# A three-part feed-forward kernel: gate weights loaded ahead of the down weights, up-weight sums moved beside the down product, three low parts moved from GpSimd to VectorE

## The reference, cut to what matters

```python
h = x + jnp.concatenate([pool_o, attn_o], axis=-1) @ w_out
hn = rms_norm(h, norm_ffn)
return h + (jax.nn.silu(hn @ w_gate) * (hn @ w_up)) @ w_down
```

## Time and profile before

| | |
|---|---|
| median of 3 runs | 2499.61 us (2497.76 to 2503.51) |
| profiled execution, its own time | 2495.08 us |
| span of its trace | 2493.3 us |
| busy share PE, DVE, ACT, POOL | 88%, 59%, 35%, 39% |
| mean granted TensorE clock | 0.947 |

### The profile page before, as it was taken

How to read it: one execution, slowest core, us unless ns; L and a number is a source line. 1 busy time by engine, 2 the same in 40 slices (tenths; PEclk the granted TensorE clock), 3 DMA queues, 4 the chain that set the end, 5 groups by cost and what they waited for, 6 DMA issues and landing times.

```text
span 2493.3 us, 33524 instructions
## 1 busy us (share of the span) xinstructions
PE 2186.0 (88%) x12454; PEld 1963.1 (79%) x12454; DVE 1477.0 (59%) x2118; ACT 884.4 (35%) x2149; POOL 974.1 (39%) x597
## 2 busy tenths in 40 slices
PE   7999999979999798888868888888886988889888
PEld 6888888758778787787767787787875878878877
DVE  5555665531235566666667666666667566656665
ACT  5666666422352223223223222223223332322221
POOL 1000000322254455445546444455545545544452
PEclk9999999989999899999989899999998999999999
DMA  5111110336552221122224212221113322112221
GB/s 162 35 37 37 44 38 22 102 110 197 191 181 79 85 68 51 51 76 68 60 74 144 74 51 62 75 68 51 51 60 118 112 63 68 52 51 62 74 68 64
DMA packets 236730, 195.59 MB, mean 78 GB/s; under 512 B 20749, under 2 KB 216122, under 8 KB 236570
## 3 DMA queue, kind: packets, MB, share of 16 engines
q1 hardware_dynamic: 236570, 193.46, 25.4%
HBM read 158.50 MB, written 35.03 MB: 78 GB/s over the span
## 4 chain that ended last, share of the span: by engine, by line
PE 57%; DMA 12%; DVE 11%; issue 11%; ACT 5%; SPq 2%; POOL 1%; ACTq 0%; DVEq 0%
PE ps L750 16%; PE ps L751 15%; PE ps L752 15%; DMA w_lo_raw<-in_w_gate 10%; DVE ws_lo_raw L1424 3%; PE ps L846 2%; DVE act_lo L1495 2%; SPq L438 2%; PE ps L820 1%; DVE aa L1485 1%; ACT w_hi L1167 1%; PE ps L941 1%; PE ps L832 1%; DVE act_hi L1493 1%; ACT act_hi L1202 1%
## 5 line engine op out<-in xcount | busy, mean ns | idle before, releaser
L750 PE MATMUL ps<-xs_hi,w_hi 128*128 128x352 f32 x1848 | 637.1, 345 | 228.9 <-DVE u L1459 115.0
L678 POOL TENSOR_TENSOR w_lo<-w_lo_raw,w_hi 128x512 fp32r<-128x512 f32 (+1 forms) x264 | 456.5, 1739 | 814.9 <-DVE ws_lo_raw L1424 733.5
L752 PE MATMUL ps<-xs_lo,w_hi 128*128 128x352 f32 x1848 | 624.6, 338 | 0.0
L750 PEld LDWEIGHTS ps<-xs_hi,w_hi 128*128 128x128 f32 x1848 | 373.6, 202 | 253.7 <-issue 151.0
L678 POOL TENSOR_TENSOR ws_lo<-ws_lo_raw,w_hi 128x512 fp32r<-128x512 f32 x264 | 392.0, 1495 | 63.9 <-DVE ws_lo_raw L1424 41.5
L1559 DVE TENSOR_TENSOR h<-ps,h 128x512 f32<-128x512 f32 (+1 forms) x396 | 272.4, 690 | 216.3 <-PE ps L752 213.9
L752 PEld LDWEIGHTS ps<-xs_lo,w_hi 128*128 128x128 f32 x1848 | 373.1, 202 | 0.0
L751 PE MATMUL ps<-xs_hi,ws_lo 128*128 128x352 f32 x1056 | 353.0, 334 | 0.0
L1424 DVE TENSOR_TENSOR ws_lo_raw<-w_lo_raw 128x512 f32<-128x512 f32 x132 | 201.6, 1527 | 178.7 <-DMA w_lo_raw<-in_w_gate 174.5
L750 PE MATMUL ps<-w_hi,act_hi 128*128 128x512 f32 x660 | 259.0, 392 | 25.9 <-issue 23.7
L751 PE MATMUL ps<-xs_hi,w_lo 128*128 128x352 f32 x792 | 271.2, 342 | 0.0
(11 more groups left out here) (125 smaller groups left out, 3376.0 us busy)
## 6 DMA issues: line engine op xcount, KB each, us to landing
w_lo_raw<-in_w_gate SPq DMA_DIRECT2D x66, 512.0 KB, 7.0
w_lo_raw<-in_w_up SPq DMA_DIRECT2D x66, 512.0 KB, 5.1
w_lo_raw<-in_w_down SPq DMA_DIRECT2D x66, 512.0 KB, 4.2
xload<-in_x_prompt SPq DMA_DIRECT2D x16, 512.0 KB, 4.2
mix_d<-o_st SPq DMA_DIRECT2D x64, 128.0 KB, 1.8
xt_lo_raw<-mix_d SPq DMA_DIRECT2D x16, 512.0 KB, 6.3
wg_hi_raw<-in_x_prompt SPq DMA_DIRECT2D x16, 512.0 KB, 6.8
h_d<-wg_hi_raw SPq DMA_DIRECT2D x16, 512.0 KB, 2.8
```

The costliest lines, as they stand in the source:

```text
L678: nc.gpsimd.tensor_tensor(lo, raw, hi.bitcast(F32), ALU.subtract).then_inc(done, 1)
L750: nc.tensor.matmul(out, s_hi, m_hi, start=first, stop=False, skip_group_check=partial)
L752: return nc.tensor.matmul(out, s_hi, m_lo, start=False, stop=final, skip_group_check=partial)
```

## The change

1. SP: from the second group of a part on, the gate weights of the next group (`load_gate_up(2G+2)`) are issued ahead of `load_down(G)` instead of behind it.
2. VectorE: the four weight sums of an up set leave `gate_sums` and go between the adds of `accumulate`, beside the down product (not where the gate set is the first of a part). `gate_sums` keeps five additions.
3. ScalarE: in a gate set the four silus come first, and then all seven `high2` of the up set, instead of one by one in turn (again not in the first set of a part).
4. VectorE for GpSimd: the low parts m = 0, 1, 2 of a gate set are made by VectorE (`weight_low`), inside `activations` of the up set before. GpSimd makes m = 3 to 6, and waits ahead of them until all seven products of that up set are done. Then it makes the low parts of the down weights, and then those of the next up set.

```diff
+def low_on_dve(s, m):
+    return m < 3 and s % 2 == 0 and s % (2 * GROUPS) > 0
...
@@ sync
                     if j == 0:
                         store_y(p - 1)
+                    elif G + 1 < NG:
+                        load_gate_up(2 * G + 2)
                     load_down(G)
...
                 if j == GROUPS - 1 and p + 1 < PARTS:
                     load_first_halves(p + 1)
-                if G + 1 < NG:
+                if j == 0:
                     load_gate_up(2 * G + 2)
...
@@ gpsimd
-            for s in range(SETS):
-                G, which = divmod(s, 2)
+            for G in range(NG):
                 p, j = divmod(G, GROUPS)
+                if j > 0:
+
+                    pool.wait_ge(product_done, after_product(2 * G - 1, PRODUCTS - 1))
+                    for m in range(3, PRODUCTS):
+                        low2(2 * G, m)
+                    low1(G - 1)
                 for m in range(PRODUCTS):
-                    if s + 1 < SETS:
-                        low2(s + 1, m)
-                    if m == 2 and which == 1:
-                        low1(G)
-                if which == 1 and j == GROUPS - 1 and p + 1 < PARTS:
+                    low2(2 * G + 1, m)
+                if j == GROUPS - 1:
+                    low1(G)
+                if G + 1 < NG:
+                    for m in range(PRODUCTS if j == GROUPS - 1 else 0):
+                        low2(2 * G + 2, m)
+                if j == GROUPS - 1 and p + 1 < PARTS:
                     for m in X_LOWS_POOL:
                         rows_low(p + 1, m)
...
@@ tensor
             def product(s, m):
                 p = s // (2 * GROUPS)
-                pe.wait_ge(w2_split, PRODUCTS * s + m + 1)
+                pe.wait_ge(w2_split_dve if low_on_dve(s, m) else w2_split, W_LOW[s, m] + 1)
...
@@ scalar
+                for n in range(4):
+                    if s == 0 and n < 2:
+                        stage_copy(NTILES - 1, n)
+                    gate(G, n)
+                    if j == 0:
+                        high2(s + 1, n + 3)
+                if j > 0:
+                    for m in range(PRODUCTS):
+                        high2(s + 1, m)
...
@@ vector
+            def weight_low(s, m):
+
+                dve.wait_ge(w_sum, 4 * s + m + 1)
+                dve.wait_ge(w2_high, PRODUCTS * s + m + 1)
+                nc.vector.tensor_tensor(low_of(s, m), raw_of(s, m), w2_hi[:, m].bitcast(F32), ALU.subtract)\
+                    .then_inc(w2_split_dve, 1)
...
             def gate_sums(s):
+
+                now = s % (2 * GROUPS) == 0
                 q7_sum(s)
-                weight_sum(s + 1, 0)
+                if now:
+                    weight_sum(s + 1, 0)
                 u2_sum(s)
...
                 q7_sum(s)
+                lows = more and not new_part
                 if more:
                     weight_sum(s + 1, 0)
+                if lows:
+                    weight_low(s + 1, 0)
                 u2_sum(s)
                 if more:
                     weight_sum(s + 1, 1)
+                if lows:
+                    weight_low(s + 1, 1)
+                if more:
                     weight_sum(s + 1, 2)
                 act_product(G, 0)
+                if lows:
+                    weight_low(s + 1, 2)
...
                 for j in range(PT_TILES):
+                    if group < GROUPS - 1 and j < 4:
+                        weight_sum(2 * G + 3, j)
                     rows = part_rows(p, j)[0]
```

More of the change, by code:

```diff
@@ L1 @@
+import itertools
 from contextlib import ExitStack
@@ L73 @@
 RESULTS = ((0, 0), (1, 1), (1, 0), (0, 1))
+def low_on_dve(s, m):
+    return m < 3 and s % 2 == 0 and s % (2 * GROUPS) > 0
+W_LOWS = {on: [e for e in itertools.product(range(SETS), range(PRODUCTS)) if low_on_dve(*e) == on]
+          for on in (False, True)}
+W_LOW = {e: i for lows in W_LOWS.values() for i, e in enumerate(lows)}
 X_HIGHS = (0, 1, 4, 2, 3, 5, 6)
@@ L350, in build @@
         w2_split = sem("w2_split")
+        w2_split_dve = sem("w2_split_dve")
         w1_high = sem("w1_high")
@@ L1273, in _ @@
             nc.scalar.preload_act_table(ACT.Silu)
-            for s in range(SETS):
-                G, which = divmod(s, 2)
+            for G in range(NG):
                 p, j = divmod(G, GROUPS)
+                s = 2 * G
                 save_p1(s)
-                for m in range(3):
-                    if s + 1 < SETS:
+                if j == 0:
+                    for m in range(3):
                         high2(s + 1, m)
-                if which == 1:
-                    high1(G)
+                for n in range(4):
+                    if s == 0 and n < 2:
+                        stage_copy(NTILES - 1, n)
+                    gate(G, n)
+                    if j == 0:
+                        high2(s + 1, n + 3)
+                if j > 0:
+                    for m in range(PRODUCTS):
+                        high2(s + 1, m)
+                s = 2 * G + 1
+                save_p1(s)
+                if G + 1 < NG:
+                    for m in range(3):
+                        high2(s + 1, m)
+                high1(G)
                 if s == 1:
@@ L1285, in _ @@
                 for n in range(4):
[L1286 to L1292, removed]
+                    high_part(G, n)
+                    if G + 1 < NG:
                         high2(s + 1, n + 3)
-                if which == 1 and j == GROUPS - 1 and p + 1 < PARTS:
+                if j == GROUPS - 1 and p + 1 < PARTS:
                     for m in X_HIGHS:
@@ L1498, in gate_sums @@
             def gate_sums(s):
+                now = s % (2 * GROUPS) == 0
                 q7_sum(s)
-                weight_sum(s + 1, 0)
+                if now:
+                    weight_sum(s + 1, 0)
                 u2_sum(s)
-                weight_sum(s + 1, 1)
-                weight_sum(s + 1, 2)
+                if now:
+                    weight_sum(s + 1, 1)
+                    weight_sum(s + 1, 2)
                 result_sum(s, 1)
-                weight_sum(s + 1, 3)
+                if now:
+                    weight_sum(s + 1, 3)
                 result_sum(s, 2)
```

## The result

The changed kernel takes 2196.31 us (median, 2195.91 to 2203.0) against 2501.17 us for the kernel before on the same chip (2497.76 to 2503.51): a ratio of 0.8788, 95% interval 0.8768 to 0.8809. The forecast was 2221 us with a range from 2202 to 2264, so the direction and most of the size were right, and the kernel was faster than the range allowed.

A forecast was written before the change was run, and what follows sets the result against it. TensorE, busy 88% of the span, was taken as the bound, with some 300 us of stalls. Gains of 247.5 + 16 + 15 = 278.5 us from 2495.1 give 2216.6, plus 4.5 to the median: 2221 us, range 2202 to 2264.

The forecast's parts named there:

- Double blocks: The 27 double blocks: 36.67 us each falls to 27.5 us (26.9 + 0.6), 247.5 us gained in all.
- the rule of turns: Late in a double block, GpSimd and VectorE alternate, each VectorE step waiting behind a GpSimd instruction; `u2` at 21.8, wanted 21.2.
- no `u2` stall at all: Bound of the main forecast's own range: without the 0.6 us `u2` stall in double blocks, 16 us less.
- Single blocks: Two single blocks, waiting up to 11.4 us for the gate load: 8 us each gained, 16 in all; bounds 0 and 23.
- Triple blocks: Three triple blocks, 141.4 us: late middle gate load stays, 15 us of the 33.7 us excess gained; bounds 5 and 25.
- The floor of 107.7 us: Triple blocks' needed time: three sets need 40.4 us and two 26.9, 107.7 in all, leaving an excess of 33.7.
- `save_p1` without a stall: Gate set of a double block: `save_p1` ends at 18.8, product 3 wants it at 19.2; the 3.53 us stall goes.
- second case: Rival: VectorE's chain one GpSimd instruction longer, `u2` stall 1.85 instead of 0.6 us per double block, 2255 us; chance 0.27.
- third case: Rival: only the 115.0 us of `u2` waits go, low parts on VectorE cost what they save, 2385 us; chance 0.05.
- The clock did not fall: Rival: denser PE work gets the lower clock level; 557 us more at it would lose the 278 us; chance 0.02.
- cost 0: Up set's four weight sums and high parts beside the 15.5 us down: they fit before the up set starts, cost 0.
- no gap of 3 us is left: Double blocks: the clock is at full level because no gap of 3 us remains.

## Why the prediction was wrong, point by point

The forecast of the median was 24.7 us too high (2221 against 2196.3). By the terms of the sum:

- **Double blocks**, forecast 247.5 us, measured 264.2: 16.7 us too little. The step that failed is this one: "VectorE has the two steps of the last low part, each behind a GpSimd instruction, until 20.9, then q and `u2` at 21.8 ... a stall of 0.6 us." In the trace only the first of the two steps is held up (0.68 us at 1347.22, then 0.51 at 1347.82), they are done at 18.6, and `u2` waits for its product: no double block has a stall. The evidence was at hand: the earlier trace rows stop one line short of the same two steps in the kernel before, which last 0.65 and 0.51 us there. I had carried the rule of turns on without reading them. The bound of "no `u2` stall at all", 16 us, was the case that came true.

```profile
1244.77 0.65 DVE L1493 TENSOR_TENSOR act_hi<-aa,act_hi 128x64 fp32r<-128x64 f32 x1 [0.56 <-ACT act_hi L1202]
1245.34 0.51 DVE L1495 TENSOR_TENSOR act_lo<-aa,act_hi 128x352 fp32r<-128x352 f32 x1
```

- **Single blocks**, forecast 16 us, measured 19.3, within the bounds.
- **Triple blocks**, forecast 15 us, measured 14.3. The late gate load in their middle set stayed, as said. The floor of 107.7 us was too low: the window of the first block holds 192 matmuls (x194 in the earlier trace rows, which counts matmuls at its edges too), sixteen products or 30.7 us and not two sets of 26.9, so the excess was 29.9 us and not 33.7. The 15 us was a share taken by judgement from a wrong excess, and that it came within 1 us is partly luck.
- **Downs and the rest**: forecast unchanged, 0.9 us less in the span.
- **From the profiled execution to the median**: I added 4.5 us because the kernel before's profiled execution lay so far under its median; the changed kernel's lies on it (2196.35 against 2196.31).
- **The range**: 16.7 + 3.3 - 0.7 + 0.9 + 4.5 = 24.7. Its lower end, 2202, took the first of these in full (2221 - 16 = 2205) and next to nothing of the others. The prediction says that it takes in the bounds of the single and the triple blocks; it does not. With their 7 and 10 us the bounds reach down to 2188.

What was right: the block explained as 26.9 us of products, idle time and clock; the early load hidden by the down; the load as the first stall; `save_p1` without a stall (18.8 forecast, 18.3 measured, 19.2 wanted); the low part at the sum's duration. The second case, one turn more, did not come (the copy has 0.9 us to spare, not 0.4). The third, only the load's wait goes, was 2385 us; that edit alone gives 2352. The clock did not fall: 0.983 over the run.

What was wrong in the reasons, though it did not cost much in the sum: I put the end of the later stalls down to GpSimd being held idle for 13.7 us and named that as the argument against the third case. The hold is worth nothing (2199.5 us without it), nor are the three low parts on VectorE (2200.0 without either). It was the order on GpSimd, with the two long subtractions last (about 105 us), and the sums beside the down together with ScalarE's order, which I entered as "cost 0" and which are worth about 50 us. The walk through the row had both in it, but I did not ask of each edit what the row would be without it.

The rule of the Trainium skill that was weighed (Perfetto Trace Analysis, Optimizing Scalar/DVE Operations: moving work between GpSimd and VectorE might not help) came true for the three low parts: 2197.5 us with them on GpSimd, 2196.3 with them on VectorE. As a third case it still failed, since the time came from other edits.

## What to carry to other kernels

Where VectorE's chain sets when TensorE goes on, look at what GpSimd runs beside its operations with two SBUF inputs, and put GpSimd's longest instructions where VectorE reads from PSUM; here the order of two subtractions was worth more than moving three from one engine to the other. A load that waits for an early event must not stand in the queue behind one that waits for a late event. When a change has several edits, walk the row once without each of them, and when several terms of a sum have one-sided bounds, add the bounds up before the range is set.

## What the runs showed of the hardware

- A VectorE operation with both inputs in SBUF and a GpSimd subtraction hold each other up: 0.52 us became 2.72 beside a 128x1024 subtraction, while the adds into h, with one input in PSUM, lasted 0.69 us beside GpSimd and without it. The Trainium skill (SBUF — State Buffer, Who interferes with whom) says that a VectorE instruction with two SBUF inputs contends with a GpSimd instruction that reads SBUF, and that one with at most one SBUF input, outside the 2-port modes, does not; the trace agrees on both. The new part is what follows the blocked one: a short VectorE operation of 0.21 us that had waited was followed by the next at its full speed (0.68, then 0.51 us), and GpSimd's next subtraction took longer beside it (1.63 us instead of 1.30). In this place a turn cost less than one wait per operation.
- The clock falls behind some gaps of about 2.7 us and not behind others: in the kernel with the down weights' low parts first, equal gaps gave blocks of 29.8 and of 31.4 us, mostly in turn. So the prediction's "no gap of 3 us is left" was not the condition for full clock; it held because no gap at all was left. With the load put back, one block with a gap of 3.0 us kept full clock and one with 2.7 us had 0.95. Gaps of 1.36 us (sums back in the gate set) left every block at 1.00. In the blocks of the kernel before with a gap of 3.5 us the clock was 0.91 to 0.95.
- Loads of 512 KB landed 5.2 us after their issue (median of the gate loads after the change), and 7.0 us in the kernel before, where each was issued right behind the down load.
